# The last two token blocks of a product-key expert layer: gathered expert rows against both whole expert tables in matrix products

## The reference

```python
def peer(x, w_q, keys_1, keys_2, expert_u, expert_v):      # x is x1; u and v are 16384 x 1024
    def block(xb):                                         # 128 tokens
        q = (xb @ w_q).reshape(TOKEN_BLOCK, PEER_HEADS, 2, PEER_HALF)
        s1 = jnp.einsum('thd,hkd->thk', q[:, :, 0], k1)    # 8 heads, 128 keys
        s2 = jnp.einsum('thd,hkd->thk', q[:, :, 1], k2)
        v1, i1 = lax.top_k(s1, PEER_TOPK)                  # 16
        v2, i2 = lax.top_k(s2, PEER_TOPK)
        cand_s = v1[..., :, None] + v2[..., None, :]
        cand_i = i1[..., :, None] * N_KEYS + i2[..., None, :]
        top_s, pos = lax.top_k(cand_s, PEER_TOPK)
        idx = jnp.take_along_axis(cand_i, pos, axis=-1)
        gate = jax.nn.softmax(top_s, axis=-1)
        u, vv = expert_u[idx], expert_v[idx]
        act = jax.nn.gelu(jnp.einsum('td,thkd->thk', xb, u))
        return jnp.einsum('thk,thkd->td', gate * act, vv)
    x = layer_norm(DEEPNORM_ALPHA * x + y_peer, ln2_g[l], ln2_b[l])
```

## Time and profile before

| What | Value |
|---|---|
| median of 3 runs | 3086.72 us |
| the profiled execution, its span | 3085.0 us |
| median less span (launch and end, outside the span) | 1.7 us |
| TensorE busy, with matmuls | 67% |
| VectorE busy | 75% |
| ScalarE busy | 37% |
| GpSimd busy | 43% |
| moved by DMA | 1172 MB, mean 380 GB/s |

### The profile page before, as it was taken

One profiled execution on the slowest core, in us unless ns is written; L12 is line 12 of the kernel. 1 busy time (PEld: TensorE's weight loads), 2 busy tenths in 40 slices (PEclk: granted clock), 3 DMA queues, 4 the chain that ended last, 5 costly groups with the idle time before them and its releaser, 6 DMA issues. The chain is left out here.

```text
span 3085.0 us, 54203 instructions
## 1 busy us (share of the span) xinstructions
...
## 2 busy tenths in 40 slices
...
PEclk9999989888987877789989888875555555555555
...
GB/s 163 60 64 137 275 413 405 419 416 409 415 421 417 419 417 420 417 421 421 419 420 410 420 421 421 419 419 419 418 419 418 418 420 419 417 417 419 417 419 303
DMA packets 167847, 1172.07 MB, mean 380 GB/s; under 512 B 18357, under 2 KB 18485, under 8 KB 31034
## 3 DMA queue, kind: packets, MB, share of 16 engines
q0 software_dynamic: 147456, 1073.81, 84.1%
q1 hardware_dynamic: 20154, 95.01, 7.9%
...
## 5 line engine op out<-in xcount | busy, mean ns | idle before, releaser
L727 POOL DMA_INDIRECT arena_high<-uv_dram,idx_now x1024 | 1273.4, 1244 | 1381.9 <-PE ps L1002 1196.2
L2033 DVE SCALAR_TENSOR_TENSOR arena_high<-arena_low,arena_high 128x1024 f32<-128x1024 f32 x1024 | 1242.2, 1224 | 581.1 <-DMA arena_high<-uv_dram,idx_now 572.3
L1002 PE MATMUL ps<-arena_high 32*32 32x512 f32 x16384 | 820.5, 835 | 937.3 <-ACT arena_high L1489 933.3
L1480 ACT ACTIVATE gcol<-hcol 128x2 f32<-128x2 f32 x512 | 104.0, 203 | 1581.6 <-DVE arena_high L2033 1581.3
L1002 PEld LDWEIGHTS ps<-arena_high 32*32 32x32 f32 x16384 | 136.6, 119 | 1483.0 <-ACT arena_high L1489 1402.9
L1489 ACT ACTIVATE arena_high<-arena_high,wcol 128x32 f32<-128x32 f32 x1024 | 272.9, 313 | 16.7
L963 PE MATMUL ps<-arena_low 128*128 128x512 f32 (+1 forms) x512 | 253.2, 637 | 0.2 <-issue 0.2
L1482 ACT ACTIVATE wcol<-gcol,arena_high 128x1 f32<-128x1 f32 x1024 | 245.6, 287 | 16.9
L722 POOL CAST idx_now<-arena_high 128x8 uint32<-128x8 f32 x128 | 62.4, 488 | 209.1 <-DVE arena_high L2019 208.6
L963 PEld LDWEIGHTS ps<-arena_low 128*128 128x128 f32 x512 | 101.9, 213 | 168.8 <-issue 159.2
L1141 PE MATMUL ps<-arena_low 128*128 128x512 f32 x256 | 126.0, 638 | 0.0
...
...
## 6 DMA issues: line engine op xcount, KB each, us to landing
...
arena_high<-uv_dram,idx_now POOLq DMA_INDIRECT x1024, 12.5
arena_low<-w_mix_dram SPq DMA_DIRECT2D x8, 1536.0 KB, 11.5
arena_high<-w_proj_dram SPq DMA_DIRECT2D x16, 512.0 KB, 3.2
...
arena_low<-w_proj_dram SPq DMA_DIRECT2D x16, 512.0 KB, 11.7
arena_high<-w_mix_dram SPq DMA_DIRECT2D x8, 512.0 KB, 7.0
arena_high<-w_out_dram SPq DMA_DIRECT2D x2, 2048.0 KB, 9.6
```

Source lines behind the costliest of these rows:

```text
L727: pool.indirect_dma_start(out=ring[:, s % RING, :], out_offset=None, in_=uv_d, in_offset=bass.IndirectOffsetOnAxis(ap=idx_now[:, s:s + 1], ...
L1002: last = nc.tensor.matmul(ps[out:out + QUAD, y_bank(t // PH) + turn, :], diag[rows, s % DIAGS, :], ring[rows, s % RING, cs], start=fresh, ...
L1480: steps.link(nc.scalar.activation(gcol[:, s0:s0 + 2], hcol[:, s0:s0 + 2], ACT.Gelu))
L2033: last = nc.vector.scalar_tensor_tensor(out=ring[:, s % RING, 0:D], in0=x1[c][:, j, :], scalar=1.0, in1=ring[:, s % RING, 0:D], op0=ALU.mu ...
```

## The change

The last two blocks of the order (6 and 7, DENSE = 2) no longer gather. TURNS falls from 64 to 48. For those two blocks the kernel computes, beside turns 35 to 47:

- **picks**: the same search by `dense_pick` on VectorE, 16 heads of blocks, each in 4 steps, from step 256 to 319; the results (two indices and a gate for each of 128 picks of a token) stay in `picks`.
- **u phase**, steps 284 to 336 (U_STEPS = 53): all of u, transposed on the host (`ut_d`), in 128 tiles of 512 KB through 6 slots; each tile is 8 float32 matmuls 256 wide (both blocks at once) with 128 x 128 weights; gelu of all 16384 x 256 products (`dense_act`), stored to DRAM in 16 chunks of 1 MB (`act_d`). In steps 320 to 335 also the **gates as a matrix**: for each token two one-hot rows (`hot_group`, 8 VectorE instructions 128 wide for 4 tokens) and one matmul that adds up gate by pair of keys (`g_group`), stored to DRAM in 16 pieces of 1 MB (`g_d`).
- **v phase**, steps 337 to 383 (V_STEPS = 47): for each of 16 chunks the gelus and the gates come back (`load_chunk`, the gates in runs of 512 bytes), are multiplied and split into high and low parts; all of v in 128 tiles of 512 KB through 4 slots, each rounded by ScalarE, its rest taken by VectorE, then 12 matmuls 512 wide as split products, accumulated over all tiles in banks 4 to 7.
- **end**: `dense_finish` norms each of the two blocks after the gathered ones.

The slabs 13 to 19 come one in 4 steps from step 256 on (`paced_slab`), two for each turn, in two buffers. The semaphores of earlier stages are used again with an offset (`wait_again`). Every block's sums now use banks 0 to 3, and the merge is at step 0 of a turn for all blocks. In each engine's list the step's dense work stands in this place: on TensorE ahead of `experts` of the same step; on ScalarE and VectorE at the end of the step, behind `expert_weights` and `dots`.

```diff
+DENSE = 2
+GB = NB - DENSE
-TURNS = NB * PH
+TURNS = GB * PH
...
-    return t - 30 + LATE_SLAB if 30 <= t < 30 + PH + ALONE_LATE else None
+    return t - 30 + LATE_SLAB if 30 <= t < 32 else None
+def paced_slab(G):
+    i, o = divmod(G - 32 * STEPS, PACE)
+    return (PACED + i, o) if 0 <= i < len(SLABS) - PACED else (None, o)
+PACE = 4
+PACED = LATE_SLAB + 2
+U0 = 32 * STEPS + PACE * (len(SLABS) - PACED)
+U_STEPS = 53
+V_STEPS = TURNS * STEPS - U0 - U_STEPS
+PICK0 = 32 * STEPS
+PICK_PARTS = 4
+NT = NKEY
+CH = 8
+USLOTS = 6
+G_STEP0 = PICK0 + DENSE * PH * PICK_PARTS - U0
+def u_first(s):
+    return NT * s // U_STEPS
+def v_first(v):
+    return NT * v // V_STEPS
+def w_step(c):
+    return U_STEPS + max(v for v in range(V_STEPS) if v_first(v) <= c * CH) - 1
+def dense_head(k):
+    return (1 + k // DENSE) % PH
...
+            def load_u(n):
+                if n == 0:
+                    sp_eng.wait_ge(score_psum, len(SLABS))
+                if n >= USLOTS:
+                    wait_again(sp_eng, u_used, n - USLOTS + 1)
+                sp_eng.dma_start(u_slot[n % USLOTS].rearrange("p a b -> p (a b)"), ut_d[n, :, :]).then_inc(u_in[n % USLOTS].sem, 16)
+            def store_act(c):
+                wait_again(sp_eng, act_ready, CH // 2 * (c + 1))
+                sp_eng.dma_start(act_d[c, :, :], act_out[c % 2].rearrange("p a b -> p (a b)")).then_inc(act_stored[c % 2].sem, 16)
+            def store_g(i):
+                wait_again(sp_eng, g_read, 4 * (i + 1))
+                sp_eng.dma_start(g_d[i, :, :], g_out[i % 2].rearrange("p a b -> p (a b)")).then_inc(g_stored[i % 2].sem, 16)
+            def load_v(n):
+                if n < 4:
+                    wait_again(sp_eng, u_used, (NT - 1 - n) // USLOTS * USLOTS + n + 1)
+                else:
+                    wait_again(sp_eng, v_used, n - 3)
+                sp_eng.dma_start(v_raw[n % 4], uv_d[n * P:(n + 1) * P, D:2 * D]).then_inc(v_in[n % 4].sem, 16)
+            def load_chunk(c):
+                if c == 0:
+                    for i in range(2):
+                        wait_again(sp_eng, act_stored[i], 16 * NT // CH // 2)
+                        wait_again(sp_eng, g_stored[i], 16 * 16 // 2)
+                if c >= 2:
+                    wait_again(sp_eng, v_used, CH * (c - 1))
+                src = g_d[:, :, c * CH * 16:(c + 1) * CH * 16].rearrange("a p b -> p a b")
+                sp_eng.dma_start(g_in[c % 2], src).then_inc(chunk_in[c % 2].sem, 16)
+                sp_eng.dma_start(act_in[c % 2].rearrange("p a b -> p (a b)"), act_d[c, :, :]).then_inc(chunk_in[c % 2].sem, 16)
...
+            for n in range(NT):
+                load_u(n)
+                if n % CH == 0 and n >= 2 * CH:
+                    store_act(n // CH - 2)
+                for i in range(16):
+                    if n == u_first(G_STEP0 + i + 1) + USLOTS:
+                        store_g(i)
+                if n == u_first(41 * STEPS - U0 + 1) + USLOTS:
+                    store_out(BLK)
+            store_act(NT // CH - 2)
+            for i in range(16):
+                if u_first(G_STEP0 + i + 1) + USLOTS >= NT:
+                    store_g(i)
...
+            for n in range(4):
+                load_v(n)
+            store_act(NT // CH - 1)
+            load_chunk(0)
+            load_chunk(1)
+            for n in range(4, NT):
+                if n % CH == 4 and CH < n < NT - CH:
+                    load_chunk(n // CH + 1)
+                load_v(n)
...
+            def u_tile(n):
+                if n == 0:
+                    pe.wait_ge(q_ready, 2 * len(SLABS))
+                if n >= 4 and n % 2 == 0:
+                    wait_again(pe, act_ready, n // 2 - 1)
+                wait_again(pe, u_in[n % USLOTS], 16 * (n // USLOTS + 1))
+                o = n % 2 * 2 * P
+                for k in range(KD):
+                    last = nc.tensor.matmul(ps[:, 4 + n % 4 // 2, o:o + 2 * P], u_slot[n % USLOTS][:, k, :],
+                                            x1T[:, BLK - DENSE:BLK, k, :], start=(k == 0), stop=(k == KD - 1),
+                                            skip_group_check=True)
+                last.then_inc(u_used.sem, 1)
+            def g_group(i):
+                wait_again(pe, hot_ready, i + 1)
+                if i == 0:
+                    wait_again(pe, picks_ready, 1)
+                if i >= 2:
+                    wait_again(pe, g_read, i - 1)
+                for q in range(4):
+                    last = nc.tensor.matmul(ps[:, 6 + i % 2, q * P:(q + 1) * P], hot[:, i % 2, q, 0:P],
+                                            hot[:, i % 2, q, P:2 * P], start=True, stop=True, skip_group_check=True)
+                last.then_inc(g_psum.sem, 1)
+            def v_tile(n):
+                if n == 0:
+                    wait_again(pe, act_ready, NT // 2)
+                    wait_again(pe, g_read, GROUPS)
+                if n % CH == 0:
+                    wait_again(pe, w_low, n // CH + 1)
+                wait_again(pe, v_lo_done, n + 1)
+                c, i = n // CH, n % CH
+                for j in range(DENSE):
+                    js = slice(j * P, (j + 1) * P)
+                    for h in range(2):
+                        hs = slice(h * HALF, (h + 1) * HALF)
+                        last = split_products(ps[:, 4 + 2 * j + h, :], (w_hi_c[c % 2][:, i, js], w_lo_c[c % 2][:, i, js]),
+                                              (v_hi_r[n % 4][:, hs], v_lo_r[n % 4][:, hs]), n == 0, n == NT - 1)
+                last.then_inc(v_used.sem, 1)
...
+                if s == G_STEP0:
+                    turn_picks()
+                if 0 <= s < U_STEPS:
+                    for n in range(u_first(s), u_first(s + 1)):
+                        u_tile(n)
+                if G_STEP0 <= s < G_STEP0 + 16:
+                    for i in range(4 * (s - G_STEP0), 4 * (s - G_STEP0) + 4):
+                        g_group(i)
+                v = s - U_STEPS
+                if 0 <= v < V_STEPS:
+                    for n in range(v_first(v), v_first(v + 1)):
+                        v_tile(n)
...
+                i, o = paced_slab(t * STEPS + g)
+                if i is not None and o < PACE - 1:
+                    for k in range((0, 5, 11)[o], (5, 11, 16)[o]):
+                        queries_chunk(i, k // KD, k % KD, k % KD + 1)
+                if i is not None and o == PACE - 1:
+                    scores(i)
...
+            def dense_act(n):
+                c, i = n // CH, n % CH
+                wait_again(act, u_used, n + 2)
+                if i == 0 and c >= 2:
+                    wait_again(act, act_stored[c % 2], 16 * (c // 2))
+                nc.scalar.activation(act_out[c % 2][:, i:i + 2, :].rearrange("p a b -> p (a b)"), ps[:, 4 + n % 4 // 2, :],
...
+            def round_v(n):
+                wait_again(act, v_in[n % 4], 16 * (n // 4 + 1))
+                if n == 0:
+                    wait_again(act, u_used, NT - 2)
+                nc.scalar.activation(v_hi_r[n % 4], v_raw[n % 4], ACT.Copy).then_inc(v_rounded.sem, 1)
...
+                v = s - U_STEPS
+                if -1 <= v < V_STEPS:
+                    for n in range(v_first(v) + 2 if v >= 0 else 0, min(v_first(v + 1) + 2, NT)):
+                        round_v(n)
...
+            def dense_finish(j):
+                pb, y = GB + j, dense_y[j]
+                wait_again(dve, v_used, NT)
+                nc.vector.scalar_tensor_tensor(out=y, in0=x1[1][:, pb - BLK, :], scalar=ALPHA,
+                                               in1=ps_flat[:, (4 + 2 * j) * HALF:(6 + 2 * j) * HALF],
+                                               op0=ALU.mult, op1=ALU.add).then_inc(y_read, 1)
+                dve.wait_ge(y_read, pb + 1)
+                norm_stats(y, Steps(dve, ln2_step, pb * 2), var2_ready)
+                norm_centre(y, ln2_g_bc, var2_ready, pb)
+                norm_rstd(Steps(dve, ln2_step, pb * 2 + 1), std2_ready, pb)
+                norm_scale(y, y, ln2_b_bc).then_inc(out_ready, 1)
...
+            def hot_group(i):
+                if i == 0:
+                    wait_again(dve, picks_ready, 1)
+                if i >= 2:
+                    wait_again(dve, g_psum, i - 1)
+                j = i // (P // 4)
+                for q in range(4):
+                    t = 4 * i + q - j * P
+                    nc.vector.tensor_scalar(hot[:, i % 2, q, 0:P], iota128[:, :], picksT[:, j, 1, t:t + 1], None, ALU.is_equal)
+                    last = nc.vector.tensor_scalar(hot[:, i % 2, q, P:2 * P], iota128[:, :], picksT[:, j, 0, t:t + 1],
+                                                   picksT[:, j, 2, t:t + 1], ALU.is_equal, ALU.mult)
+                last.then_inc(hot_ready.sem, 1)
...
+                now = [c for c in range(NT // CH) if s == w_step(c)]
+                for c in now:
+                    wait_again(dve, chunk_in[c % 2], 32 * (c // 2 + 1))
+                    a = act_in[c % 2].rearrange("p i (b t) -> p i b t", t=16)
```

(12 more changed lines are left out.)

256 lines of the change are left out of this document (209 added, 47 removed).

## The result

The kernel before took 3086.95 us (median of 4 runs), the changed one 3258.18 us (4 runs, 3254.86 to 3266.75): a ratio of 1.0558, 95% interval 1.0543 to 1.0573. Two expert tables read whole, for two token blocks, cost 171 us more than gathering the rows that these blocks need. The profiled execution has a span of 3257.8 us.

A forecast was written before the change was run, and what follows sets the result against it. Transfers bound the kernel before; TensorE was to bound the u phase, waits the v phase. 1756.8 + 168 + 6 + 628 + 25 + 611 + 25.5 = 3220 us of span, so 3222 us; range 3055 to 3350.

The forecast's parts named there:

- Two shares: From step 284: DMA share near 0.8 beside TensorE 95% busy or more; then, in the v phase, TensorE near 65%.
- Steps 256 to 283: Before the u phase: VectorE with the picks and DMA about level, 6.0 us a step, 168 us (160 to 180).
- much over 6 us: Sign that the prediction is wrong: steps 256 to 283 taking much over 6 us each.
- To step 256: Start of the kernel: nothing changes but names and one 128-wide copy, 1756.8 us.
- The u phase: 53 steps bound by TensorE, 11.8 us a step, transfers hidden: 628 us (585 to 680).
- From u to v: Last gelu, store, chunk loads, product and rounding in sequence: 29 us, taken as 25 (15 to 40).
- The v phase: 47 steps paced by waits, taken as 13.0 us a step: 611 us (480 to 710).
- the chain through the order of the lists: v phase: load, rounding, rest, dots and matmuls wait in turn, 22.2 to 26.0 us in two steps, 11.1 to 13.0 each.
- the other loop that the prediction had priced: v phase: `load_v(n)` waits for tile n - 4, so 3.2 to 4.2 us a tile, 8.8 to 11.4 a step.
- Bytes and packets: v phase floor: 477 us by bytes; 560 us if 512-byte packets cost 0.05 us each, extrapolated from two rows.
- full transfers: Rival, chance 0.22: in the v phase loads land in time, it runs near its bytes; kernel 3048 us.
- Waits add up: Rival, chance 0.13: chunk loads hold VectorE and the clock falls, v step 15.0 us, u phase 660; kernel 3369 us.

The follow-up runs named there:

- Experiment 1: Changed kernel with the loads of slabs 14 and 15 ahead of the store of block 3 in SyncE's list: 3227.76 us, ratio to before 1.0452.
- experiment 6: Changed kernel with those slab loads ahead of the store and U_STEPS 70 instead of 53, four v slots: 3185.39 us, ratio to before 1.0322.
- experiment 4: Changed kernel with six slots for v tiles instead of four, still rounding two tiles ahead: 3155.29 us (one run).
- experiment 7: Changed kernel with slab loads before the store, U_STEPS 70, six v slots, lookahead 4, chunk 0 loaded earlier, two gate groups a step over 32 steps: 3045.36 us.
- experiment 8: The kernel of experiment 7 with v tiles rounded two ahead instead of four: 3107.49 us, ratio to before 1.007.
- 9: The kernel of experiment 7 with v tiles rounded three ahead instead of four: 3070.01 us, ratio to before 0.9937.
- experiment 3: Changed kernel with gates loaded in rows of 8 KB instead of 512-byte runs, same bytes but wrong gates: 3229.12 us (one run).

## Why the prediction was right, and where it wasn't

The side, the size and the range held: 3222 predicted, 3258 measured, slower by 5.6% where 4.4% was said. Both halves of the argument stand. TensorE takes over in the u phase, and the v phase is paced by waits for tiles of 512 KB. But the closeness of the v phase is luck, since its number came from a chain that doesn't set it, and one step is missing. Two shares were off as well: DMA stood at 0.91 in the u phase, not near 0.8, at 346 GB/s, so a share of DMA time moved fewer bytes than the 420 GB/s that the sum used; and TensorE was busy for 76% of the v phase, not 65%, some of it at a lower clock.

**Steps 256 to 283** is the term that failed. The prediction said 6.0 us a step and looked at VectorE and the bytes; it named no queue for this part. It moved the slabs' due times and never moved their loads past what stands in SyncE's list. The row that told it was there to be read in the trace of before: the load at 1800.68 behind the store at 1800.30, in turn 32. Experiment 1 measured 26 us for it in the trace and 30.4 in the medians. The rest of the term, 12 us, is a step of 6.4 us on average, 7.2 in the first eight steps with TensorE busy for most of them, an engine that the term didn't price; what makes them long wasn't tried. The prediction had named a step "much over 6 us" as a sign that it is wrong, and with the stop it was 7.4.

**To step 256** came 6.2 us late. The twelve traces of the changed kernel and its edits, which are the same program up to there, reach step 256 between 1756.4 and 1770.5 us, so this is the spread of single executions.

**The u phase**: passes 256 wide were to stand 0.227 us apart. The timeline of TensorE in it (L1417 `u_tile`, L1430 the gate groups), as the earlier trace rows for the kernel before:

```profile
2303.27 7.17 PE L1417 MATMUL ps<-arena_low 128*128 128x256 f32 x32
...
2397.34 1.95 PE L1430 MATMUL ps<-arena_low 128*128 128x128 f32 x16
2400.39 1.16 PE L1430 MATMUL ps<-arena_low 128*128 128x128 f32 x8 [1.10 <-DVE arena_low L2429]
2402.20 1.87 PE L1430 MATMUL ps<-arena_low 128*128 128x128 f32 x8 [0.65 <-DVE arena_low L2429]
```

(7.17 - 0.17) / 32 = 0.219 us: the interpolation was 4% high. The tiles took 453 us of the phase instead of 465, the gate groups 69 instead of 62, the experts 58 as said, and TensorE's idle time was 29 instead of 25: together what the 610 of the prediction had. The 15 us by which the term was too large are the 18 added for the clock, which was 0.99 and not 0.96. The waits of the third and fourth gate group are there, 1.10 and 0.65 us before the matmuls.

**From u to v**: 31.4 us. The chain was named right and its first number, 29 us, too; the cut to 25 "with the queues empty" was the mistake. SyncE's and VectorE's timelines (L798 `store_act`, L821 and L822 the two loads of a chunk, L2448 its product, L2458 its low part):

```profile
2589.12 0.51 SPq L798 DMA_DIRECT2D acts_dram<-arena_low  x1
2601.69 0.38 SPq L821 DMA_DIRECT2D arena_low<-spread_dram  x1
2602.11 2.15 SPq L822 DMA_DIRECT2D arena_low<-acts_dram  x1
...
2610.74 2.29 DVE L2448 TENSOR_TENSOR arena_low<-arena_low 128x2048 f32<-128x2048 f32 x1 [31.68 <-DMA arena_low<-acts_dram]
...
2615.22 2.28 DVE L2458 TENSOR_TENSOR w_lo_bytes<-arena_low,w_hi_bytes 128x2048 fp32r<-128x2048 f32 x1
```

The store took 2601.69 - 2589.12 = 12.6 us, since it is 1 MB and had been counted as 512 KB (9.1); three v tiles go out in front of it at 2587.79, so the queues weren't empty. The loads took 8.6, less than the 12.7 counted; that the two errors nearly cancel is luck.

**The v phase**: 13.07 us a step against 13.0. The number came from the chain through the order of the lists (11.1 to 13.0 a step), and this chain isn't what sets the time: with 30 steps it would have given 390 us or less, and experiment 6 gave 535. What sets it is nearer to the other loop that the prediction had priced, four slots with one landing in them (3.2 to 4.2 us a tile), and set aside as the lower one. Measured, it is 4.80 a tile with four slots and 3.99 with six. The trace gives the round of a slot, as the mean of tiles 16 to 123:

| part of the round, us | predicted | changed kernel |
|---|---|---|
| from the load's issue to its landing | 7.9 to 11.7 | 8.65 |
| until ScalarE begins to round | 0 | 2.04 |
| rounding, rest (and between them) | 2.28 | 2.56 |
| until TensorE begins | 0 | 2.43 |
| the matmuls | 2.7 | 3.35 |
| until the next load goes out | 0 | 0.58 |
| sum, and a tile by four slots | 12.9 to 16.7, 3.2 to 4.2 | 19.6, 4.9 |

The landing was well priced. What the loop lacked is some 5 us in which a tile, or its slot, waits for an engine to come to it in its list, and matmuls that are longer, in part by a clock of 0.88. A freed slot gets its next load after 0.6 us, so the ring is nearly always full, and experiment 4 shows that its size holds the phase. Slots aren't all, though: at 4.3 tiles a step two more of them (with the other edits of experiment 7 and a lookahead of 2) brought only 21 us, and it took the lookahead of 4 for the other 68. Slots, lookahead and tiles a step act together; a lookahead shorter than the tiles of a step leaves the next one to be rounded in the same step, and a longer one lets ScalarE wait for landings with other work behind it. Both are seen in the traces at experiments 8 and 9. A lookahead of 3 with 2.7 tiles a step wasn't tried.

**Bytes and packets**: the line through two kinds of packets gave 0.05 us for 512 bytes and a floor of 560 us; experiment 3 has 0.03, so the floor lies nearer to the other end: 9 ns for each of 32,768 packets on 16 engines are 18 us, and 477 + 18 = 495 us. The two rows of the line are means over packets of 4 bytes to 16 KB, and 128 packets of 704 bytes in the trace of before took 38 ns each where the line has 56. The Trainium skill, "DMA: Bandwidth & Descriptors", section Specifications, which puts the least size for line rate at 512 bytes, was the closer of the two; that section names no price for such a packet, which here was 9 ns over its bytes. The section Bandwidth of that page asks for 1 MiB for 75% of peak; the u phase of experiment 7 has tiles of 512 KB beside gathers at a DMA share of 1.01 and 412 GB/s, so here the trace decides against that rule for transfers that are queued behind each other.

**The rivals**: *full transfers* needed a v step of 10.1 to 11.3 us. With six slots it was 10.9, and the kernel took 3155; without the stop at the slab that would be some 3125, still slower than before. Experiment 7 came to 3045 us, beside the 3048 that this rival was priced at, but it is another kernel and has other terms (598 + 26 + 446 instead of 592 + 15 + 490), so the likeness is chance. *Waits add up* named VectorE held by a chunk; with four slots and 2.7 tiles a step VectorE's only wait there was 31.7 us, the first, so it was wrong for this kernel. In experiment 8 VectorE did wait for chunks, 111 us, and yet the kernel gained only 6.6 us when the product was moved.
